# A delta rule loop of two steps a turn, with buffers by parity in place of copies

## The chip, the cores and the metric

The kernel runs on one core of one Trainium2 chip. The metric is the device time of one execution in microseconds; the median of several runs is given. TensorE is the matmul engine (PE in the profile, PEld for its weight loads), VectorE is DVE, ScalarE is ACT, GpSimd is POOL, and SyncE (SP) issues the DMAs of the part that is changed.

## What is computed

One layer of a bidirectional sequence mixer, followed by an MLP, over 2048 latent tokens with a prefix of 256 context tokens. The change touches one of the mixer's two head groups, the gated delta rule with 8 heads of width 64. It is computed in chunks of 64 tokens, for a forward and a backward direction:

```
gam = cumsum(log_g); dec = exp(gam_i - gam_j) for i >= j
a = (beta k) k^T * dec_strict + I                  # per chunk, 64 x 64
u = a^-1 (v beta); w = a^-1 (beta k exp(gam))
qk = (q k^T) * dec_incl
def step(s, xs):                                   # 36 chunks one after the other
    v_new = u - w s
    o = (q exp(gam)) s + qk v_new
    s = g_last * s + (k exp(gam_last - gam))^T v_new
```

The 256 context tokens and the 2048 latent tokens together make 36 chunks (NCH) in each direction.

## The kernel before

The program runs its phases one after the other: input norm and modulation, the input projection, the delta rule (`phase_gdn`), the other head group (HGRN), and then merge, output projection and MLP. Each engine has its own instruction list, and they synchronise by semaphores; within an engine everything runs in the order of its list.

`phase_gdn` handles one chunk a step, for all 8 heads and both directions at once, in tiles of 128 partitions by 512 numbers of fp32 (`W`). A matmul group in it is 16 matmuls of 64x64x64 in the code; the profile lists each group as 32 matmuls and 32 weight loads. The inverse of the triangular matrix is grown by levels: a `product` (a transposition of the inverse so far, and N times the inverse) on TensorE, a `take` from PSUM to SBUF on ScalarE (`g_txs`), a `grown` on TensorE, and a masked copy into the inverse on VectorE (`grow_block`, COPY_PREDICATED). Levels 0, 1 and the product of level 2 belong to the step n of the chunk; the rest of level 2, and levels 3 and 4 (`late_product`, `late_take`, `late_grown`, `late_block`), are done for chunk m = n - 1 while chunk n runs its early levels. Beside them, chunk m has its state work: `kv` (transposes keys and values), `ks` and `qs` (keys and queries times the state), `tz` (the inverse times the residual), `kdvn` (the update of the state) and `amvn` (the output).

Because two chunks are in work at once, ScalarE copies what chunk n+1 would overwrite: `nn` to `nn2` (hand_nn), `tt` to `tt2` (hand_tt), `tt2` to `ttb` (keep_inverse), values out of PSUM to `vt` (vtake), and `am` to `amb` (keep_am, three instructions, two of which also swap partition halves). GpSimd prepares the decay factors of chunk n+1 (`gaps`, `seeds`) from `grow`, a row that SyncE fetches with four DMAs (`load_rows`).

The steps are driven by `steps`: bodies 0, 35 and 36 are written out, and bodies 1 to 34 are one body in a loop (`eng.Fori(0, NCH - 2)`) with one step a turn. Every engine has its own copy of this loop, and waits in it compare a semaphore with a register that grows with the turn (`at`).

The names that the texts below use: in the profile, L1077, L1087, L1097, L1107, L1118 and L1129 are the matmuls of the helpers `to_tokens`, `to_channels`, `turn`, `across`, `back` and `keyed`.

Of the kernel before, what the change touches and what calls it, by code (L numbers as in the profile page):

```python
# [926 lines left out]
def at(i, n0, per, c):  # L927

    return n0 * per + c if i is None else i * per + (n0 * per + c)


def phase_gdn(nc, e):

    with nc.cleanup_on_exit(), ExitStack() as ctx:
# [11 lines left out]
        kqa, kqvb = sb("g_kqa", [P, 2, 2, PAIRS, CH]), sb("g_kqvb", [P, 2, 3, PAIRS, CH])  # L946
# [3 lines left out]
        nn, nn2, tt, tt2, ttb, am, amb = (sb("g_" + n, [P, *W]) for n in ("nn", "nn2", "tt", "tt2", "ttb", "am", "amb"))  # L950
        txs, txs2 = sb("g_txs", [P, 2, *W]), sb("g_txs2", [P, 2, *W])
        kd, vt, z, vn, o1, o, s, s1 = (sb("g_" + n, [P, *W]) for n in ("kd", "vt", "z", "vn", "o1", "o", "s", "s1"))
# [11 lines left out]
        nn2_ready, tt2_ready, ttb_ready, amb_ready = sem("g_nn2"), sem("g_tt2"), sem("g_ttb"), sem("g_amb")  # L964
        z_half, z_ready, o1_ready, o_ready, s_ready = sem("g_zh"), sem("g_z"), sem("g_o1"), sem("g_o"), sem("g_s")
        vt_ready, vn_ready, exp_ready, s1_ready = sem("g_vt"), sem("g_vn"), sem("g_exp"), sem("g_s1")
# [29 lines left out]
        def steps(eng, first, body):  # L996

            first()
            body(None, 0, True, False, True)
            with eng.Fori(0, NCH - 2) as i:  # L1000
                body(i, 1, True, True, True)
            body(None, NCH - 1, True, True, False)
            body(None, NCH, False, True, False)

        def chunks(i, n):

            if i is None:
                return n, NCH + CCH - 1 - n
            return i + n, i * (-1) + (NCH + CCH - 1 - n)

        with nc.Block() as block:
            @block.sync
            def _(sp):
# [15 lines left out]
                def load_kqvb(i, n):  # L1029
                    for g in range(2):  # L1030
                        src = e.skqv[:, ds(chunks(i, n)[g], 1)]
                        sp.dma_start(kqvb[:, g].rearrange("p (c j) a t -> p c (j a t)", c=1),
                                     src.rearrange("p c j t -> p c (j t)")).then_inc(kqvb_in, 16)
# [6 lines left out]
                def first():  # L1040
# [10 lines left out]
                    load_kqa(None, 0)  # L1051

                def body(i, n, a, c, pre):
# [15 lines left out]
            def _(pe):  # L1069
# [103 lines left out]
                def body(i, n, a, c, pre):  # L1173
                    m = n - 1

# [8 lines left out]
                    def product(l):  # L1184
# [7 lines left out]
                        turn(side(pa, 1), tile(tt))  # L1192
                        to_channels(side(pa, 0), tile(nn), tile(tt)).then_inc(tx_done, 1)
# [7 lines left out]
                    def late_product(l):  # L1201

                        pe.wait_ge(pred2_done, at(i, m, 3, l - 2))
                        pe.wait_ge(nn2_ready, at(i, m, 1, 1))
                        pe.sem_inc(go, 1)
                        turn(side(pc, 1), tile(tt2))
                        to_channels(side(pc, 0), tile(nn2), tile(tt2)).then_inc(tx2_done, 1)
# [13 lines left out]
                    def kv():  # L1221
                        pe.wait_ge(kqvb_in, at(i, m, 32, 32))
                        pe.wait_ge(s_ready, at(i, m, 1, 1))
                        pe.sem_inc(go, 1)
                        turn(side(pd, 0), chan(kqvb, 0), 1)
                        turn(side(pd, 1), chan(kqvb, 2)).then_inc(kv_turned, 1)

                    def ks():
                        pe.wait_ge(o_ready, at(i, m, 1, 1))
                        pe.sem_inc(go, 1)  # L1230
                        to_tokens(side(pb, 0), chan(kqvb, 0), of_state).then_inc(ks_done, 1)

                    def qs():
                        pe.wait_ge(vt_ready, at(i, m, 1, 1))
                        pe.sem_inc(go, 1)
                        to_tokens(side(pd, 0), chan(kqvb, 1), of_state, False).then_inc(qs_done, 1)

                    def tz():
                        pe.wait_ge(pred2_done, at(i, m, 3, 3))
                        pe.wait_ge(z_ready, at(i, m, 1, 1))  # L1240
                        pe.sem_inc(go, 1)
                        across(side(pb, 1), tile(ttb), tile(z)).then_inc(tz_done, 1)
# [11 lines left out]

                    if a:
                        gram()
                    if c:
                        kv()
                        late_grown(2)
                        late_product(3)  # L1260
                    if a:
                        product(0)
                    if c:
                        late_grown(3)
                        ks()
                    if a:
                        grown(0)
# [3 lines left out]
                    if a:  # L1271
                        product(1)
                    if c:
                        late_grown(4)
                    if a:
                        grown(1)
                    if c:
                        tz()
                    if a:
                        product(2)  # L1280
                    if c:
                        kdvn()
# [4 lines left out]
            def _(act):  # L1287
# [31 lines left out]
                def body(i, n, a, c, pre):  # L1319
# [10 lines left out]
                    def keep_am():  # L1330
# [3 lines left out]
                        nc.scalar.activation(amb[:, :, 0:2, :], am[:, :, 0:2, :], ACT.Copy)  # L1334
                        nc.scalar.activation(amb[halves(1), :, 2:4, :], am[halves(0), :, 2:4, :], ACT.Copy)
                        nc.scalar.activation(amb[halves(0), :, 2:4, :], am[halves(1), :, 2:4, :], ACT.Copy).then_inc(amb_ready, 1)
# [7 lines left out]
                    def hand_nn():  # L1344
                        act.wait_ge(nn_ready, at(i, n, 1, 1))
                        if c:
                            act.wait_ge(tx2_done, at(i, m, 2, 2))
                        nc.scalar.activation(nn2[:, :, :, :], nn[:, :, :, :], ACT.Copy).then_inc(nn2_ready, 1)

                    def hand_tt():  # L1350
                        act.wait_ge(pred_done, at(i, n, 2, 2))
                        nc.scalar.activation(tt2[:, :, :, :], tt[:, :, :, :], ACT.Copy).then_inc(tt2_ready, 1)

                    def vtake():
                        act.wait_ge(kd_ready, at(i, m, 1, 1))
                        nc.scalar.activation(heads_first(vt), pd[:, :, 1], ACT.Copy).then_inc(vt_ready, 1)
# [5 lines left out]
                    if c:  # L1362
                        keep_am()
                        vtake()
                        late_take(3)
                    if a:
                        take(0)
                    if pre:
                        distances(i, n + 1)
                    if c:  # L1370
                        keep_inverse()
                    if pre:
                        decays(i, n + 1)
                    if c:
                        late_take(4)
                    if a:
                        take(1)
                        hand_nn()
                    if c:
                        vntake()  # L1380
                    if a:
                        hand_tt()
# [4 lines left out]
            def _(pool):  # L1387
                def gaps(i, n):
                    nc.gpsimd.tensor_copy(cola[:, :, :, :].unsqueeze(2), colq[:, 0:3, ds(i + n if i is not None else n, 1)])\
# [17 lines left out]
                def take_colb(i, n):  # L1407
                    st = i + n if i is not None else n
# [12 lines left out]
                def body(i, n, a, c, pre):  # L1421
                    m = n - 1
                    if c:
# [3 lines left out]
                    if a:  # L1427
                        pool.wait_ge(tt_half, at(i, n, 1, 1))
# [1923 lines left out]
```

## Time and profile before

| | us |
|---|---|
| median of 3 runs (3765.59 to 3772.26) | 3768.53 |
| the profiled execution, its own time | 3773.59 |
| its span | 3771.8 |
| delta rule phase, bodies 0 to 36 (1081 to 1703) | 622 |
| of it the loop of one step a turn from its second turn on (1121.0 to 1660.9) | 539.9 |

The span is what the profile of one execution covers; the time of that execution is 1.8 us longer. Over the span the matmuls are busy for 87% of the time, VectorE for 53%, ScalarE for 44% and GpSimd for 45%. In the delta rule phase no engine is above 80%. A count such as x32 in a row of the timeline is the number of matmuls merged into it, "idle before" is how long the engine had nothing to do ahead of the row, and what stands behind the arrow is what ended that idle time; "issue" there means that the profile shows nothing that the engine waited for.

### The profile page before, as it was taken

How to read it: one execution, taken by the hardware profiler on the slowest of the kernel's cores; microseconds unless marked ns; L12 is line 12 of the kernel's file. 1: busy time of each engine (PE TensorE's matmuls, PEld its weight loads, DVE VectorE, ACT ScalarE, POOL GpSimd, SP SyncE). 2: the span in 40 equal slices, each digit the busy share in tenths (PEclk: the TensorE clock that was granted, in tenths of full speed). 3: DMA queues.
4: the chain of work that ended last, by engine and by line, in shares of the span. 5: the costliest groups of instructions: out<-in, count | busy, mean ns of one | idle time of the engine just before them, and what ended most of it. 6: DMA issues, size and time to landing. Idle time of an engine off the chain costs nothing. (4 is left out here: it accounts for less than half of the span.)

```text
span 3771.8 us, 114554 instructions
## 1 busy us (share of the span) xinstructions
PE 3270.4 (87%) x49145; PEld 2736.9 (73%) x49145; DVE 1995.1 (53%) x2896; ACT 1669.3 (44%) x2453; POOL 1715.4 (45%) x1364
## 2 busy tenths in 40 slices
PE   6899999999968788775677566999999999999998
PEld 3677888888857777764666535878877887787877
DVE  5488510111025555555666667665565546657575
ACT  5566422442135565552444424564454453323243
POOL 0211222333035555532666337546646656656564
PEclk8899999999979999995877867999999999999999
DMA  5133443353233333324433365766675666645453
GB/s 199 48 68 73 101 101 95 107 139 114 70 99 112 112 114 113 109 86 116 114 103 91 134 211 183 234 228 197 199 249 173 204 204 248 245 161 220 177 223 123
DMA packets 438348, 555.94 MB, mean 147 GB/s; under 512 B 119788, under 2 KB 355664, under 8 KB 413656
## 3 DMA queue, kind: packets, MB, share of 16 engines
q1 hardware_dynamic: 411936, 514.10, 42.7%
q10 hardware_dynamic: 20536, 21.58, 1.7%
q0 software_dynamic: 5632, 16.78, 1.5%
q8 instruction: 180, 2.95, 0.3%
q14 instruction: 64, 0.52, 0.0%
HBM read 354.42 MB, written 197.97 MB: 146 GB/s over the span
## 5 line engine op out<-in xcount | busy, mean ns | idle before, releaser
L3015 PE MATMUL o_pg<-o_t_hi,o_s_hi 128*128 128x512 f32 x2016 | 793.4, 394 | 47.1 <-ACT o_part L3062 13.0
L3017 PE MATMUL o_pg<-o_t_lo,o_s_hi 128*128 128x512 f32 x2016 | 790.2, 392 | 0.0
L3018 PE MATMUL o_pg<-o_t_hi,o_s_lo 128*128 128x512 f32 x2016 | 789.9, 392 | 0.0
L600 PE MATMUL p_pg<-h_hi,p_whi 128*128 128x512 f32 (+1 forms) x1384 | 531.6, 384 | 9.5 <-DVE p_wlo L827 9.5
L600 PE MATMUL p_pg<-h_lo,p_whi 128*128 128x512 f32 (+1 forms) x1384 | 519.4, 375 | 0.0
L600 PE MATMUL p_pg<-h_hi,p_wlo 128*128 128x512 f32 (+1 forms) x1384 | 519.3, 375 | 0.0
L3015 PEld LDWEIGHTS o_pg<-o_t_hi,o_s_hi 128*128 128x128 f32 x2016 | 381.8, 189 | 137.7 <-DVE o_s_lo L3222 35.7
L3018 PEld LDWEIGHTS o_pg<-o_t_hi,o_s_lo 128*128 128x128 f32 x2016 | 381.9, 189 | 80.1
L3017 PEld LDWEIGHTS o_pg<-o_t_lo,o_s_hi 128*128 128x128 f32 x2016 | 381.7, 189 | 78.7
L3222 DVE TENSOR_TENSOR o_s_lo<-o_raw,o_s_hi 128x512 fp32r<-128x512 f32 x288 | 267.5, 931 | 202.6 <-ACT o_s_hi L3051 202.6
L600 PEld LDWEIGHTS p_pg<-h_hi,p_whi 128*128 128x128 f32 x1384 | 262.4, 190 | 61.0 <-DVE p_wlo L827 9.8
L600 PEld LDWEIGHTS p_pg<-h_lo,p_whi 128*128 128x128 f32 x1384 | 262.5, 190 | 51.2 <-issue 5.5
L600 PEld LDWEIGHTS p_pg<-h_hi,p_wlo 128*128 128x128 f32 x1384 | 262.2, 189 | 47.0
L3051 ACT ACTIVATE o_s_hi<-o_raw 128x512 fp32r<-128x512 f32 x288 | 179.9, 625 | 227.4 <-PE o_pg L3018 215.0
L3222 DVE TENSOR_TENSOR o_s_lo<-o_mix,o_s_hi 128x512 fp32r<-128x512 f32 x216 | 209.2, 968 | 123.5 <-ACT o_s_hi L3051 123.5
L2948 POOL TENSOR_TENSOR o_xf<-o_xf,o_part 128x512 f32<-128x512 f32 x90 | 158.4, 1760 | 252.0 <-DVE o_part L3212 206.8
L808 ACT ACTIVATE p_y<-p_pg 128x512 f32<-128x512 f32 (+1 forms) x108 | 96.7, 895 | 379.0 <-PE p_pg L600 294.1
L674 POOL TENSOR_SCALAR p_macc<-p_mw,sc 128x512 f32<-128x512 f32 x8 | 13.7, 1717 | 530.7 <-PE p_pg L620 528.4
L3051 ACT ACTIVATE o_s_hi<-o_mix 128x512 fp32r<-128x512 f32 x216 | 135.4, 627 | 213.3 <-PE o_pg L3018 199.3
L2931 POOL TENSOR_TENSOR o_mix<-o_raw 128x512 f32<-128x512 f32 x72 | 101.2, 1406 | 188.7 <-DVE o_s_lo L3222 131.1
L1932 PE MATMUL b_pf<-b_qp,b_ks 64*64 64x32 f32 x3072 | 142.9, 252 | 49.4 <-ACT b_ax L2047 30.3
L823 DVE TENSOR_TENSOR p_wlo<-p_raw,p_whi 128x1024 fp32r<-128x1024 f32 x37 | 48.1, 1300 | 244.3 <-ACT p_whi L693 241.0
(334 smaller groups left out, 6669.3 us busy)
## 6 DMA issues: line engine op xcount, KB each, us to landing
o_raw<-in_w_mlp SPq DMA_DIRECT2D x32, 1024.0 KB, 6.4
scr_f<-o_xf SPq DMA_DIRECT2D x64, 512.0 KB, 8.1
o_raw<-scr_f SPq DMA_DIRECT2D x32, 1024.0 KB, 5.3
scr_w<-o_pre SPq DMA_DIRECT2D x16, 1792.0 KB, 7.1
o_t_raw<-scr_w SPq DMA_DIRECT2D x28, 1024.0 KB, 4.9
g_kqvb<-scr_kqv SPq DMA_DIRECT2D x72, 384.0 KB, 3.5
o_xf<-scr_x SPq DMA_DIRECT2D x22, 1024.0 KB, 7.7
p_raw<-in_w_in SPq DMA_DIRECT2D x38, 512.0 KB, 5.8
```

The lines of the kernel that those rows point to most:

```text
L600: last = nc.tensor.matmul(pg[0:m, bank, 0:n], w[:, q, k, 0:m], h[bank][:, k, :], start=(k == 0 and j == 0), stop=(k == KT - 1 and j == 2))
L674: nc.gpsimd.tensor_scalar(macc[:, :], w, sc, None, ALU.mult).then_inc(m_part, 1)
L808: last = nc.scalar.activation(put(yrow[u]), src, f)
L823: dve.tensor_tensor(wlo[:, q, :, 0:m], raw[:, q, :, 0:m], whi[:, q, :, 0:m].bitcast(F32), ALU.subtract).then_inc(w_lo, 1)
L1932: nc.tensor.matmul(pf[x, g, h, 0:HD // 2], ks[g][p][lo, h, x], ahead, start=True, stop=True)
L2931: nc.gpsimd.tensor_tensor(mix[:, 0], a21, a22, ALU.add).then_inc(mixed, 1)
L2948: nc.gpsimd.tensor_tensor(t, t, part[:, src], ALU.add).then_inc(x_added, 1)
L3015: nc.tensor.matmul(out, s_hi[:, q, k, :], t_hi[:, q, k, :], start=(not more and k == 0), stop=False, skip_group_check=more)
L3017: nc.tensor.matmul(out, s_hi[:, q, k, :], t_lo[:, q, k, :], start=False, stop=False, skip_group_check=more)
L3018: last = nc.tensor.matmul(out, s_lo[:, q, k, :], t_hi[:, q, k, :], start=False, stop=(k == 3), skip_group_check=more)
L3051: nc.scalar.activation(s_hi[:, q], operand(i, q), ACT.Copy).then_inc(s_hi_ready, 1)
L3222: dve.tensor_tensor(s_lo[:, q], operand(i, q), s_hi[:, q].bitcast(F32), ALU.subtract).then_inc(s_lo_ready, 1)
```

## The change

Eight edits, all in `phase_gdn`:

- The loop has two steps a turn and 16 turns. Bodies 0, 1, 34, 35 and 36 are now written out, and the loop covers 2 to 33. `at` and `chunks` count two steps a turn.
- `nn`, `tt`, `am` and `kqvb` become two buffers each, taken by the parity of the chunk. `nn2`, `tt2`, `ttb` and `vt` go, and with them four ScalarE instructions a step: hand_nn, hand_tt, keep_inverse and vtake.
- `residual_end` on VectorE subtracts the values straight from PSUM (`pd[:, :, 1]`).
- On TensorE the late level comes first in a step: `late_grown(2)` stands ahead of `gram`, `ks` ahead of `kv`, and `kdvn` ahead of `product(2)`; `grown(0)`, `product(1)` and `grown(1)` each come one place later against the late groups.
- ScalarE does `distances` and `decays` ahead of `take(0)`, and `keep_am` behind `late_take(4)`.
- GpSimd starts a step with `gaps`, and does the scaled state `s1` behind `seeds`.
- SyncE fetches `kqvb` first in a step and the decay rows `grow` two steps ahead.
- VectorE starts a step with `late_block(2)`, and `decay` waits for `tz_done` of the chunk two back, `attend` for `amb_ready` of the chunk two back.

```diff
 def at(i, n0, per, c):
-    return n0 * per + c if i is None else i * per + (n0 * per + c)
+    return n0 * per + c if i is None else i * (2 * per) + (n0 * per + c)
...
-        nn, nn2, tt, tt2, ttb, am, amb = (sb("g_" + n, [P, *W]) for n in ("nn", "nn2", "tt", "tt2", "ttb", "am", "amb"))
+        nn, tt, am = ([sb(f"g_{n}{p}", [P, *W]) for p in range(2)] for n in ("nn", "tt", "am"))
+        amb = sb("g_amb", [P, *W])
...
             first()
             body(None, 0, True, False, True)
-            with eng.Fori(0, NCH - 2) as i:
-                body(i, 1, True, True, True)
+            body(None, 1, True, True, True)
+            with eng.Fori(0, (NCH - 4) // 2) as i:
+                body(i, 2, True, True, True)
+                body(i, 3, True, True, True)
+            body(None, NCH - 2, True, True, True)
             body(None, NCH - 1, True, True, False)
             body(None, NCH, False, True, False)
...
                 def body(i, n, a, c, pre):
+                    if a:
+                        if i is not None or n > 1:
+                            sp.wait_ge(qs_done, at(i, n, 1, -1))
+                        load_kqvb(i, n)
                     if pre:
-                        sp.wait_ge(d_ready, at(i, n, 1, 1))
-                        load_rows(i, n + 1)
+                        if i is not None or n < NCH - 2:
+                            sp.wait_ge(d_ready, at(i, n, 1, 2))
+                            load_rows(i, n + 2)
                         sp.wait_ge(kkq_done, at(i, n, 1, 1))
                         load_kqa(i, n + 1)
-                    if a:
-                        if c:
-                            sp.wait_ge(qs_done, at(i, n, 1, 0))
-                        load_kqvb(i, n)
...
                     def qs():
-                        pe.wait_ge(vt_ready, at(i, m, 1, 1))
+                        pe.wait_ge(z_ready, at(i, m, 1, 1))
...
-                    def keep_inverse():
-                        act.wait_ge(pred2_done, at(i, m, 3, 2))
-                        if i is not None or m:
-                            act.wait_ge(tz_done, at(i, m, 1, 0))
-                        nc.scalar.activation(ttb[:, :, :, :], tt2[:, :, :, :], ACT.Copy).then_inc(ttb_ready, 1)
...
                     def residual_end():
                         dve.wait_ge(z_half, at(i, m, 1, 1))
-                        dve.wait_ge(vt_ready, at(i, m, 1, 1))
-                        dve.tensor_tensor(z[:, :, :, :], z[:, :, :, :], vt[:, :, :, :], ALU.subtract).then_inc(z_ready, 1)
+                        dve.wait_ge(kv_turned, at(i, m, 1, 1))
+                        dve.tensor_tensor(heads_first(z), heads_first(z), pd[:, :, 1], ALU.subtract).then_inc(z_ready, 1)
```

Three places show the instructions as they stand in the built program; the change has line numbers of its own, in which L1085, L1095, L1105, L1115, L1126 and L1137 are the matmuls of `to_tokens`, `to_channels`, `turn`, `across`, `back` and `keyed`. The first is TensorE at the end of a turn of the delta rule loop. Before, after `product(2)`, `kdvn` and `amvn` (L1129, L1118) the engine branches back; what follows is the written-out body 35:

```order
L1190 REGISTER_ALU
L1097 MATMUL g_pa<-cst,g_tt 64x64 x16
L1087 MATMUL g_pa<-g_tt,g_nn 64x64 x16
L1129 MATMUL g_pd<-g_vn,g_kd 64x64 x16
L1118 MATMUL g_pb<-g_vn,g_amb 64x64 x16
L1000 REGISTER_ALU
L1000 COMPARE_AND_BRANCH
L1077 MATMUL g_pa<-g_kqa 64x64 x32
L1097 MATMUL g_pd<-cst,g_kqvb 64x64 x32
```

In the change, the same end of a step in the middle of a turn runs on into the second step without a branch:

```order
L1199 REGISTER_ALU
L1105 MATMUL g_pa<-cst,g_tt 64x64 x16
L1095 MATMUL g_pa<-g_tt,g_nn 64x64 x16
L1126 MATMUL g_pb<-g_vn,g_amb 64x64 x16
L1221 REGISTER_ALU
L1085 MATMUL g_pc<-g_txs 64x64 x16
L1186 REGISTER_ALU
L1085 MATMUL g_pa<-g_kqa 64x64 x32
L1105 MATMUL g_pc<-cst,g_tt 64x64 x16
```

The branch stands only behind the second step, and the written-out body 34 follows it:

```order
L1199 REGISTER_ALU
L1105 MATMUL g_pa<-cst,g_tt 64x64 x16
L1095 MATMUL g_pa<-g_tt,g_nn 64x64 x16
L1126 MATMUL g_pb<-g_vn,g_amb 64x64 x16
L1003 REGISTER_ALU
L1003 COMPARE_AND_BRANCH
L1085 MATMUL g_pc<-g_txs 64x64 x16
L1085 MATMUL g_pa<-g_kqa 64x64 x32
```

A turn of this loop had 24 matmul groups on TensorE between the two ends of its branch, and has 48 now.

The second place is TensorE at the start of a step. Before, it runs `gram`, `kv`, `late_grown(2)` and `late_product(3)`:

```order
L1077 MATMUL g_pa<-g_kqa 64x64 x32
L1222 REGISTER_ALU
L1223 REGISTER_ALU
L1097 MATMUL g_pd<-cst,g_kqvb 64x64 x32
L1077 MATMUL g_pc<-g_txs 64x64 x16
L1203 REGISTER_ALU
L1097 MATMUL g_pc<-cst,g_tt 64x64 x16
L1087 MATMUL g_pc<-g_tt,g_nn 64x64 x16
```

In the change, it runs `late_grown(2)`, `gram`, `late_product(3)`, `ks` and `kv`:

```order
L1085 MATMUL g_pc<-g_txs 64x64 x16
L1186 ISA
L1085 MATMUL g_pa<-g_kqa 64x64 x32
L1212 REGISTER_ALU
L1105 MATMUL g_pc<-cst,g_tt 64x64 x16
L1095 MATMUL g_pc<-g_tt,g_nn 64x64 x16
L1235 REGISTER_ALU
L1236 ISA
L1085 MATMUL g_pb<-g_s,g_kqvb 64x64 x16
L1105 MATMUL g_pd<-cst,g_kqvb 64x64 x32
L1225 ISA
L1085 MATMUL g_pc<-g_txs 64x64 x16
```

The first group of a step is now one of 16 matmuls on `g_txs`, and `ks` (g_pb from the state) moved from behind `late_grown(3)` to ahead of `kv`.

The third place is ScalarE in the second half of a step. Before, the two takes are followed by the copy of `nn` (L1348), the take of `vn`, the copy of `tt` (L1352) and the last take:

```order
L1327 REGISTER_ALU
L1328 ACTIVATE g_txs<-g_pc 128x1024
L1323 REGISTER_ALU
L1324 ACTIVATE g_txs<-g_pa 128x1024
L1348 ACTIVATE g_nn<-g_nn 128x512
L1360 ACTIVATE g_vn<-g_pb 128x512
L1351 REGISTER_ALU
L1352 ACTIVATE g_tt<-g_tt 128x512
L1323 REGISTER_ALU
L1324 ACTIVATE g_txs<-g_pa 128x1024
```

In the change, the three `amb` instructions stand between the two takes and both copies are gone:

```order
L1335 REGISTER_ALU
L1336 ACTIVATE g_txs<-g_pc 128x1024
L1339 REGISTER_ALU
L1341 REGISTER_ALU
L1343 ACTIVATE g_amb<-g_am 128x2x128
L1344 ACTIVATE g_amb<-g_am 64x2x128
L1345 ACTIVATE g_amb<-g_am 64x2x128
L1331 REGISTER_ALU
L1332 ACTIVATE g_txs<-g_pa 128x1024
L1349 ACTIVATE g_vn<-g_pb 128x512
L1331 REGISTER_ALU
L1332 ACTIVATE g_txs<-g_pa 128x1024
```

## Rows read from the trace of the kernel before

**Rows 1.** Busy time by stretch, in us, with instruction counts and granted clock

```profile
core 0: us, PE busy (x) PEld busy (x) DVE busy (x) ACT busy (x) POOL busy (x), PEclk, DMA share, GB/s
...
1099.70:1121.00 21.30, 13.89 (x779) 12.96 (x773) 9.87 (x19) 9.86 (x15) 8.79 (x10) 0.98 0.21 66
1121.00:1660.90 539.90, 431.66 (x25287) 403.12 (x25280) 315.52 (x626) 322.65 (x494) 289.52 (x329) 1.00 0.36 112
1660.90:1683.90 23.00, 13.97 (x771) 12.75 (x771) 9.45 (x21) 9.41 (x14) 2.68 (x5) 1.00 0.16 50
```

**Rows 2.** Timeline of TensorE, one warm turn: start us, duration us, instruction

```profile
1398.87 1.16 PE L1077 MATMUL g_pa<-g_kqa 64*64 64x64 f32 x64 [0.31 <-ACT g_txs L1324]
...
1403.41 0.68 PE L1097 MATMUL g_pa<-cst,g_tt 64*64 64x64 f32 x32
...
1411.04 0.69 PE L1077 MATMUL g_pa<-g_txs 64*64 64x64 f32 x32 [0.22 <-ACT g_txs L1324]
...
1412.69 0.69 PE L1097 MATMUL g_pa<-cst,g_tt 64*64 64x64 f32 x32 [0.23 <-DVE g_tt L1487]
1413.18 0.68 PE L1087 MATMUL g_pa<-g_tt,g_nn 64*64 64x64 f32 x32
...
1415.10 1.16 PE L1077 MATMUL g_pa<-g_kqa 64*64 64x64 f32 x64 [0.31 <-ACT g_txs L1324]
```

**Rows 3.** Waits in the warm loop: total us, times, longest us

```profile
PE g_pc L1077 <- ACT g_txs L1328: 50.8, 66, 1.4
PE g_pc L1097 <- DVE g_tt L1498: 30.9, 33, 0.9
PE g_pa L1077 <- ACT g_txs L1324: 17.1, 65, 0.3
PE g_pa L1097 <- DVE g_tt L1487: 7.0, 33, 0.2
...
POOL g_dd L1395 <- DMA g_grow<-scr_gam: 127.1, 33, 4.3
```

**Rows 4.** Groups by line in the loop: busy us, mean ns

```profile
L1512 DVE TENSOR_TENSOR g_z<-g_z,g_vt 128x512 f32<-128x512 f32 x35 | 39.0, 1114 | 0.0
...
L1342 ACT ACTIVATE g_ttb<-g_tt 128x512 f32<-128x512 f32 x35 | 21.5, 615 | 2.7 <-DVE g_tt L1498 2.7
```

**Rows 5.** DMA queues of 1099:1120, 1140:1660 and 1660:1703 in turn

```profile
q8 instruction: 5, 0.08, 1.7%
...
DMA packets 62159, 58.47 MB, mean 112 GB/s; under 512 B 37839, under 2 KB 45775, under 8 KB 62159
...
q1 hardware_dynamic: 62159, 58.47, 36.5%
...
q8 instruction: 9, 0.15, 1.5%
```

**Rows 6.** Timeline of TensorE in the loop's first turn

```profile
1107.31 0.52 PE L1077 MATMUL g_pa<-g_txs 64*64 64x64 f32 x20 [0.75 <-issue]
...
1111.53 0.62 PE L1097 MATMUL g_pa<-cst,g_tt 64*64 64x64 f32 x25 [2.13 <-issue]
...
1119.12 0.69 PE L1118 MATMUL g_pb<-g_vn,g_amb 64*64 64x64 f32 x30 [1.52 <-issue]
```

**Rows 7.** Timeline of TensorE in body 35, written out behind the loop

```profile
1669.92 0.33 PE L1077 MATMUL g_pb<-g_s,g_kqvb 64*64 64x64 f32 x2 [1.30 <-issue]
1670.03 0.69 PE L1077 MATMUL g_pa<-g_txs 64*64 64x64 f32 x32
...
1671.45 0.66 PE L1077 MATMUL g_pd<-g_s,g_kqvb 64*64 64x64 f32 x28
1673.61 0.33 PE L1077 MATMUL g_pd<-g_s,g_kqvb 64*64 64x64 f32 x4 [1.49 <-issue]
...
1677.59 0.34 PE L1077 MATMUL g_pa<-g_txs 64*64 64x64 f32 x5 [0.81 <-issue]
...
1682.69 0.34 PE L1129 MATMUL g_pd<-g_vn,g_kd 64*64 64x64 f32 x7 [2.29 <-issue]
```

More of the change, by code:

```diff
@@ L945, in phase_gdn @@
         glq = sb("g_glq", [P, NCH, 2 * PAIRS])
-        kqa, kqvb = sb("g_kqa", [P, 2, 2, PAIRS, CH]), sb("g_kqvb", [P, 2, 3, PAIRS, CH])
+        kqa = sb("g_kqa", [P, 2, 2, PAIRS, CH])
+        kqvb = [sb(f"g_kqvb{p}", [P, 2, 3, PAIRS, CH]) for p in range(2)]
         grow = sb("g_grow", [P, *W])
@@ L1191, in product @@
                         pe.sem_inc(go, 1)
[L1192 to L1193 removed]
+                        turn(side(pa, 1), tile(tt[p]))
+                        to_channels(side(pa, 0), tile(nn[p]), tile(tt[p])).then_inc(tx_done, 1)
                     def grown(l):
@@ L1257, in body @@
                     if c:
-                        kv()
-                        late_grown(2)
-                        late_product(3)
+                        late_product(3)
+                        ks()
+                        kv()
+                        late_grown(3)
                     if a:
                         product(0)
[L1263 to L1267, printed above, removed]
                     if c:
@@ L1271, in body @@
                     if a:
-                        product(1)
+                        grown(0)
                     if c:
@@ L1275, in body @@
                     if a:
-                        grown(1)
+                        product(1)
                     if c:
@@ L1279, in body @@
                     if a:
+                        grown(1)
+                    if c:
+                        kdvn()
+                    if a:
                         product(2)
                     if c:
-                        kdvn()
                         amvn()
@@ L1407, in take_colb @@
                 def take_colb(i, n):
-                    st = i + n if i is not None else n
+                    st = i * 2 + n if i is not None else n
                     nc.gpsimd.tensor_copy(colb[:, :, :, :].unsqueeze(2), colq[:, Q_KDEC:Q_REST, ds(st, 1)])
@@ L1422, in body @@
                     m = n - 1
+                    if pre:
+                        gaps(i, n + 1)
+                    if a:
+                        pool.wait_ge(tt_half, at(i, n, 1, 1))
+                        pool.wait_ge(c_ready, at(i, n, 1, 1))
+                        nc.gpsimd.tensor_tensor(tt[n % 2][:, :, :, :], tt[n % 2][:, :, :, :], c2[:, :, :, :], ALU.add).then_inc(tt_init, 1)
+                    if pre:
+                        pool.wait_ge(tt_init, at(i, n, 1, 1))
+                        seeds(i, n + 1)
                     if c:
@@ L1533, in body @@
                     if a:
+                        decay()
                         attend()
                     if c:
+                        residual()
+                        late_block(3)
                         keys()
-                        late_block(3)
-                        residual()
+                        residual_end()
                     if a:
@@ L1541, in body @@
                     if c:
-                        residual_end()
+                        late_block(4)
                         carried()
-                        late_block(4)
                     if a:
```

107 lines of the change are left out of this document (39 added, 68 removed).

## The prediction, written before the change was run

> **What bounds the kernel now.** Only the delta rule phase changes, so I read the stretches of it first, from the view of busy time by stretch [rows 1]. The reader is to see three lines. The loop's first turn takes 21.3 us. The 33 turns behind it take 539.9 us, 16.36 us each. The written-out body 35 takes 23.0 us, for the same work: about 770 matmuls and 770 weight loads in all three (25287 over 33 is 766). TensorE's clock was granted in full in the last two (1.00) and nearly so in the first (0.98), and the DMA share is lowest where the step is slowest. So a step has a warm price and a cold one, some 5 to 7 us apart, and neither clock nor data traffic explains it.
>
> The second view is the timeline of one warm turn [rows 2]. From one `gram` to the next are 16.23 us (1398.87 to 1415.10). No engine is full: a matmul group occupies TensorE for 0.47 to 0.49 us (1412.69 to 1413.18), so the 24 groups are some 11.4 us. The rest are waits, and the table of waits says which: TensorE waits for the take of the late level 50.8 us in total, for the masked copy of the late level 30.9, for the early take 17.1 and for the early masked copy 7.0 [rows 3], 105.8 us or 3.2 us a turn. The warm turn is thus a chain of dependences across TensorE, ScalarE and VectorE, with the order of TensorE's list woven in. GpSimd's 127.1 us of waiting for the decay rows [rows 3] are not in that chain: `gram` waits for the last take on ScalarE in both turns shown [rows 2].
>
> The third view is the DMA queues of three stretches [rows 5], with the cold timelines beside it [rows 6, 7]. In the first turn an instruction queue (q8) moved 5 packets of 16 KB, and behind the loop 9. In 520 us of the warm loop all 62159 packets are data (q1): no code was fetched at all. And the cold timelines show what the fetch does to TensorE: it stops in the middle of a group, with nothing to wait for ("issue"), goes on, and stops again one block later. From 1669.92 to the next stop I count 2+32+32+32+28 = 126 matmuls, each with a weight load (the two groups between the rows shown are like 1670.03), so a block is some 254 instructions of these and a couple of semaphore waits. The resumptions are 11.81 us apart over three blocks in the first turn (1107.31 to 1119.12) [rows 6] and 12.77 us over three in body 35 (1669.92 to 1682.69) [rows 7]: **4.10 us a block on average**, the shortest 3.69. Blocks come one at a time and no earlier than that. Warm, TensorE goes through a block in 16.36 / 6.1 = 2.7 us. So TensorE's code is held near the engine while the loop runs, and outside it arrives slower than it is executed.
>
> **The change, part by part.** *The doubled turn.* A step is 768 / 126 = 6.1 blocks of TensorE's code. One step a turn was held; two are 12.2, and as a stretch of 12.2 rarely begins and ends at an edge, 13 blocks. Whether 13 blocks are held no row shows; this is the unknown that decides, and I bound it from both sides. Held: nothing is fetched after the first turn. Not held: if blocks leave in the order in which they came, a turn that is longer than the store finds none of its own code, and every turn is as cold as the first. I take the second. What is shown held is 6.1 blocks (7 with the edges), and 540 us of an idle fetch queue did not bring in the code behind the loop: body 35, begun at 1660.9 [rows 1], stands still until 1669.92, 1673.61, 1677.59 and 1682.69, block after block [rows 7]. A store with room for twice the loop had the time to hold it.
>
> The cold turn then costs 13 x 4.10 = 53.3 us, and I add 1 us for the branch back, since the block fetched ahead there is the one behind the loop (between 0 and a whole fetch of 4.1). That is 54.3 us for two steps. Sixteen turns: 869 us. The same 32 steps took 32 x 16.36 = 523.5. **+345 us.**
>
> The Trainium skill, "Runtime: NRT & Kernel Launch", section "Instruction fetch mechanics", gives TensorE's instruction memory as 128 KiB, 2048 instructions, a FIFO refilled in blocks of 256. By it the two steps (over 3,070 matmuls and loads) are not held and the one step was; the trace agrees with the block and with the held single step. The same section also says that there are only two lines of 16 KiB and that a branch to anything further back stalls; by that the loop before would have fetched six blocks in each turn, 25 us instead of 16.36, and here the trace contradicts it.
>
> *More written-out bodies.* Body 1 is as cold as the loop's first turn was. Body 34 was the last warm turn and is now written out: 22 us (between 21.3 and 23.0) less 16.4, **+6 us**. Bodies 0, 35 and 36 stay as they are.
>
> *The four copies.* They cost ScalarE about 0.6 us each (615 ns for `ttb`) [rows 4], 2.4 us a step, and `vtake` and the copy of `nn` stand ahead of takes that TensorE waits for. `residual_end` goes from 1114 ns [rows 4] to that of its neighbours, some 0.7. *The new order* starts the late level at once. Worth together, warm: from `product(0)` to the next `gram` are 11.69 us (1403.41 to 1415.10) [rows 2]. Without anything in their way, product and take are 2.41 (1412.69 to 1415.10) and grown and masked copy 1.65 (1411.04 to 1412.69); three of the first and two of the second are 10.53. With 0.3 for `grown(0)` behind `qs` it is 10.8, a gain of 0.85 a step. The part ahead of `product(0)` stays near 4.5 us: five groups, the masked copy between and the late take. In the cold turn all this is worth nothing: the chain of about 15.5 us a step has 27.1 us to run in, beside the stops for code. So I put it at **0**; without that cover it is -0.85 x 32 = -27.
>
> *Decay rows two steps ahead* removes GpSimd's wait, which nobody waits for: 0. The new `d_ready` wait on SyncE has the two `kqa` loads of the next chunk queued behind it, for which `gram` waits; they issue some 10 us before they are needed in so long a turn. The waits on the chunk two back (`tz_done`, `amb_ready`) are for work a whole step old: 0.
>
> Sum: +345 + 6 = +351 us on the profiled execution's 3773.6 (span 3771.8 and 1.8 around it), 4125. The median of the runs is 5.1 us lower, so **4120 us**.
>
> **The rivals.**
> 1. *All 13 blocks are held* (not slower). For it: no row shows where the store ends. Then two of 32 steps are cold and 30 warm: -0.85 x 30 = -26 us; cold steps added are 2, 3 and 34 at some 5.3 us, +16. Together -10 us, 3759 us. It decides at a single number: from 13 blocks of room upwards this holds, at 12 it does not. If the new order gains nothing, 3785, slower after all. Chance 0.12, of it 0.07 faster, 0.03 the same, 0.02 slower.
> 2. *Part is held*: something like half of the turn is kept and 6 blocks are fetched. Then a turn is 6 x 4.10 + 6.2 x 2.7 = 41.3 us against 32.7; 16 x 8.6 + 6 = +144, 3912 us. Against it: this needs a store that does not lose its blocks in order. Chance 0.06.
> 3. *The refetch as forecast*, 0.82. Its own range: at best 12.2 blocks at 3.69 and nothing at the branch, 45.0 us a turn, +197 + 5, 3970. At worst the 4.26 of body 35 and a whole fetch at the branch, 59.5 us a turn, +428 + 7, 4204; and if a third of the 3.2 us of waits for data came on top of the stops, +34 more, about 4240.
>
> **How the numbers follow.** 4120 is the refetch. 3970 to 4240 would hold it nearly always; I reach down to 3910 for the second rival, which makes some 0.82 in all. About 0.2%, 7.5 us, is what a measurement of this kernel tells from no change. Faster 0.07, same 0.03, slower 0.82 + 0.06 + 0.02 = 0.90.
>
> **What would show it.** The instruction queue should show 13 packets in each turn of the loop, some 200 where there were none; the timeline should show TensorE stopping with "issue" ahead of it, in mid-group, every 126 or so matmuls, about 4.1 us apart; the loop's 32 steps should take 870 us, at 27 us each, and no wait for a take should be the longest. ScalarE's four copies are gone, and GpSimd no longer waits for the decay rows. I am wrong if the warm turns show no instruction packets: then the time is near 3760, and the chain of takes and masked copies decides. I am wrong in size if blocks arrive faster than 3.7 us apart when they are asked for in a steady row, or if the branch back costs a fetch of its own.

## The result, and the profile after

The changed kernel takes 4178.41 us (median of 4 runs, 4176.79 to 4179.98) against 3770.4 us before in the same comparison: a ratio of 1.1082, 95% interval [1.1063, 1.1102]. It is 408 us slower. The prediction was 4120 us, in a range of 3910 to 4240.

The busy time by stretch of the changed kernel, to be read against [rows 1] (us, counts, granted TensorE clock, DMA share, GB/s): the written-out body 1, 15 turns of the loop (all but the first), body 34, body 35.

```profile
core 0: us, PE busy (x) PEld busy (x) DVE busy (x) ACT busy (x) POOL busy (x), PEclk, DMA share, GB/s
1097.90:1119.40 21.50, 15.50 (x768) 14.23 (x769) 8.47 (x18) 7.89 (x11) 8.34 (x10) 0.92 0.11 29
1172.60:2038.60 866.00, 523.43 (x23058) 484.95 (x23049) 277.03 (x570) 242.08 (x330) 251.15 (x300) 0.80 0.23 68
2039.70:2063.80 24.10, 16.61 (x768) 15.51 (x768) 9.38 (x20) 8.02 (x11) 7.16 (x8) 0.86 0.21 69
2063.80:2089.50 25.70, 15.98 (x768) 14.73 (x768) 8.39 (x20) 6.63 (x9) 3.65 (x5) 0.90 0.15 45
```

Fifteen turns take 866.0 us, 57.73 us each and 28.9 us a step, where a step took 16.36 [rows 1]. The matmuls are the same, 1537 a turn for twice 768. No turn is warm any more. A step in the loop even costs more than the cold bodies before and behind it, 28.9 us against 21.5, 24.1 and 25.7. The DMA queues of the same 15 turns:

```profile
q1 hardware_dynamic: 58560, 55.07, 21.3%
q8 instruction: 210, 3.44, 1.8%
```

These are 210 packets of code, 14 a turn, where the warm loop before had none [rows 5]. TensorE's waits in these turns (total us, times, longest):

```profile
PE g_pc L1085 <- issue: 71.4, 15, 5.0
PE g_pa L1095 <- issue: 61.7, 45, 2.4
PE g_pa L1085 <- issue: 61.6, 44, 2.3
PE g_pd L1105 <- issue: 53.6, 29, 3.6
...
PE g_pa L1105 <- DVE g_tt L1471: 11.4, 30, 0.5
PE g_pc L1085 <- ACT g_txs L1332: 8.2, 15, 0.8
```

The long waits of [rows 3], for the takes on ScalarE and the masked copies on VectorE, have shrunk to some 10 us each. In their place stands "issue", which is TensorE having no instruction. The first row is a kind of its own: it comes 15 times, once a turn, with 4.76 us each. The timeline shows both kinds; here are the first row of a turn, the rows of its second half ahead of which TensorE had stood still, and at the end the first row behind the branch back:

```profile
1294.32 1.13 PE L1085 MATMUL g_pc<-g_txs 64*64 64x64 f32 x32 [4.86 <-issue]
...
1323.98 0.58 PE L1085 MATMUL g_pa<-g_kqa 64*64 64x64 f32 x9 [1.00 <-issue]
...
1328.87 0.85 PE L1105 MATMUL g_pd<-cst,g_kqvb 64*64 64x64 f32 x42 [1.55 <-issue]
...
1332.59 0.39 PE L1095 MATMUL g_pa<-g_tt,g_nn 64*64 64x64 f32 x11 [1.62 <-issue]
...
1336.21 0.40 PE L1085 MATMUL g_pa<-g_txs 64*64 64x64 f32 x12 [1.49 <-issue]
...
1339.82 0.47 PE L1115 MATMUL g_pb<-g_z,g_tt 64*64 64x64 f32 x17 [0.82 <-issue]
...
1344.31 0.50 PE L1095 MATMUL g_pa<-g_tt,g_nn 64*64 64x64 f32 x18 [1.64 <-issue]
...
1349.98 0.50 PE L1085 MATMUL g_pc<-g_txs 64*64 64x64 f32 x8 [4.64 <-issue]
```

As in [rows 6, 7], the stops fall into the middle of groups, here 3.6 to 4.9 us apart. Then, behind the branch, TensorE stands for 4.64 us, in which it does nothing at all. That stop is the fetch of the turn's first block. The other twelve come while the turn runs: in the turn shown, the twelve distances from 1294.32 to 1344.31 are 4.17 us on average, and the last one, over the branch, is 5.67. Read in the same way over 14 turns, which are 57.8 us long on average, a turn is **12 x 4.33 + 5.8**; the 5.8 are 1.0 us of work on the last block and 4.8 of standing still. The fourteenth packet is one more than the blocks that a turn uses; I take it for the block behind the loop, fetched ahead and never used.

The rest of the change did what it says. In the groups by line GpSimd's wait for the decay rows is gone (127.1 us in [rows 3], 7.5 now, behind a copy of its own), and the subtraction straight from PSUM takes VectorE 0.68 us where the one from `vt` took 1.11 [rows 4]:

```profile
L1378 POOL TENSOR_TENSOR g_dd<-g_grow,g_cola 128x512 f32<-128x512 f32 x33 | 34.4, 1043 | 7.5 <-POOL g_cola L1372 7.4
...
L1491 DVE TENSOR_TENSOR g_z<-g_z,g_pd 128x512 f32<-128x512 f32 x35 | 23.7, 677 | 0.0
```

### The profile page after: what moved, and what is told of

Its sections match the earlier page's. It is cut to its first block and busy times, and to the rows that moved or that the text cites. A ratio compares the mean times of both kernels' runs of the same rounds, so it can differ in the third digit from the quotient of the medians.

```text
span 4175.0 us, 113800 instructions
## 1 busy us (share of the span) xinstructions
PE 3404.8 (82%) x49145; PEld 2854.8 (68%) x49145; DVE 1986.4 (48%) x2896; ACT 1605.1 (38%) x2309; POOL 1697.2 (41%) x1364
## 5 line engine op out<-in xcount | busy, mean ns | idle before, releaser
L2993 PEld LDWEIGHTS o_pg<-o_t_hi,o_s_hi 128*128 128x128 f32 x2016 | 380.9, 189 | 140.0 <-DVE o_s_lo L3200 35.9
L1332 ACT ACTIVATE g_txs<-g_pa 128x1024 f32<-128x1024 f32 x108 | 110.6, 1024 | 401.3 <-PE g_pa L1095 401.3
L1411 POOL TENSOR_TENSOR g_tt<-g_tt,g_c 128x512 f32<-128x512 f32 x36 | 46.0, 1277 | 429.0 <-DVE g_tt L1459 429.0
L1336 ACT ACTIVATE g_txs<-g_pc 128x1024 f32<-128x1024 f32 x72 | 73.8, 1025 | 292.2 <-PE g_pc L1095 292.2
```

What stands on the lines that cost most here:

```text
L1332: nc.scalar.activation(txs[:, :, :, :, :], pa[:, :, :, :, :], ACT.Copy).then_inc(tx_ready, 1)
L1336: nc.scalar.activation(txs2[:, :, :, :, :], pc[:, :, :, :, :], ACT.Copy).then_inc(tx2_ready, 1)
L1411: nc.gpsimd.tensor_tensor(tt[n % 2][:, :, :, :], tt[n % 2][:, :, :, :], c2[:, :, :, :], ALU.add).then_inc(tt_init, 1)
L2993: nc.tensor.matmul(out, s_hi[:, q, k, :], t_hi[:, q, k, :], start=(not more and k == 0), stop=False, skip_group_check=more)
```

## The experiments

### Two steps a turn and nothing else

The kernel before, with its buffers, its copies and its order, and only the loop doubled:

```diff
-            with eng.Fori(0, NCH - 2) as i:
-                body(i, 1, True, True, True)
+            body(None, 1, True, True, True)
+            with eng.Fori(0, (NCH - 4) // 2) as i:
+                body(i, 2, True, True, True)
+                body(i, 3, True, True, True)
+            body(None, NCH - 2, True, True, True)
```

> The kernel before with the two-step turn alone: one set of buffers, the four ScalarE copies and the old order of every engine kept; bodies 1 and 34 written out. Theory (TensorE's code of two steps isn't held, and each block is fetched again each turn): the turn costs what it costs in the changed kernel, 57.7 us, whatever the order in it, so 4150 to 4200 us, with 13 to 14 instruction packets a turn. Rival (a good part of the loss comes from the new order, the new waits or the parity buffers): clearly faster than the changed kernel, below 4100, and near 3790 if the doubling itself is harmless (only the written-out bodies).

Measured: 4126.79 us, ratio 1.0943 [1.0926, 1.096]. The stretch of 15 turns, and the code packets in it:

```profile
1169.20:1989.20 820.00, 493.20 (x23048) 456.40 (x23042) 296.01 (x570) 306.82 (x450) 259.13 (x300) 0.84 0.24 71
...
q8 instruction: 210, 3.44, 1.9%
```

The same 210 packets, and 54.67 us a turn. The doubling alone thus costs 355 us of the 408. The expected 4150 us was missed from below: the changed kernel has 3.06 us a turn, about 50 us, which this one has not. It does not lie at the branch. Here are the first row of a turn, its last resumption ahead of the branch and the first row behind it:

```profile
1284.33 1.98 PE L1080 MATMUL g_pa<-g_kqa 64*64 64x64 f32 x64 [4.93 <-issue]
...
1332.72 0.50 PE L1132 MATMUL g_pd<-g_vn,g_kd 64*64 64x64 f32 x17 [0.82 <-issue]
...
1338.45 1.99 PE L1080 MATMUL g_pa<-g_kqa 64*64 64x64 f32 x64 [4.71 <-issue]
```

Over the branch it is 5.73 us, as in the changed kernel, and the twelve distances ahead of it are 4.03 us on average (over 14 turns 5.8 and 4.07). So the 3 us lie in the twelve blocks that come while the turn runs, 4.33 us apart in the changed kernel and 4.07 here. The last two experiments look for the reason.

### The new order with one step a turn

The changed kernel with one set of buffers and the copies hand_nn, hand_tt and keep_inverse put back, and the loop over bodies 1 to 33. Two things stand as before the change: SyncE fetches `kqvb` last in a step, and `keep_am` comes first on ScalarE.

```diff
-            body(None, 1, True, True, True)
-            with eng.Fori(0, (NCH - 4) // 2) as i:
-                body(i, 2, True, True, True)
-                body(i, 3, True, True, True)
+            with eng.Fori(0, NCH - 3) as i:
+                body(i, 1, True, True, True)
             body(None, NCH - 2, True, True, True)
```

> The new order of all engines, decay rows two steps ahead and the subtraction straight from PSUM, but one step a turn and one set of buffers, so that three of the four ScalarE copies stay; body 34 written out. Theory (the loss is the code alone; the order is worth 0.85 us a step once the code is held): 33 warm steps save 28 us, one more cold body costs 6, about 3748 us, no instruction packets in the loop. Rival (the new order itself lengthens the step): over 3780 us. If the gain lay in the copies and not in the order, 3770 to 3780.

Measured: 3753.55 us, ratio 0.9953 [0.994, 0.9967]. 32 warm turns take 501.4 us, 15.67 each:

```profile
1118.20:1619.60 501.40, 421.92 (x24597) 395.79 (x24595) 296.90 (x608) 305.27 (x448) 269.57 (x320) 1.00 0.38 117
```

The new order, together with leaving out the take of `vt`, is a gain of 0.7 us a step once the code is held, and it needs neither the parity buffers nor the second step in a turn.

### Where the store ends: five, ten and two groups more

The kernel before, with k more matmul groups in the body of the loop; they write the same numbers to the same place:

```diff
+                        for _ in range(k if i is not None else 0):
+                            turn(side(pd, 0), chan(kqvb, 0), 1)
                         turn(side(pd, 0), chan(kqvb, 0), 1)
```

> The kernel before with five more matmul groups in the loop's body (the transposition of the keys done six times over into the same place): 29 groups instead of 24, 7.4 blocks of code instead of 6.1. Theory with a store of 8 blocks: still held, no instruction packets, and the time grows by at most 5 x 0.47 us x 34 = 80 us: 3810 to 3855 us. If the store ends below 8 blocks: every turn refetches 8 blocks and pays one more fetch at the branch, 8 x 4.1 + 4.5 = 37 us a step, +700 us, 4470.

> The same with ten more groups: 34 groups, 8.7 blocks of code. Store of 8 blocks that loses them in the order in which they came: nothing is held, 9 x 4.1 + 4.5 = 41 us a step, +820 us, about 4600, and 9 to 10 instruction packets a turn. A store of 12 blocks: held, +160 us at most, 3880 to 3930, no packets. A store that keeps a part: one to three packets a turn, 3950 to 4100.

> The kernel before with two more matmul groups in the loop's body: 26 groups, 6.6 blocks of code, which lie in 7 blocks as those of the kernel before do. Theory (held are the blocks of the loop and one ahead, 8 in all): no instruction packets, and at most 2 x 0.47 us a step, 3772 to 3805 us. Rival (the repeated transpositions themselves made the kernel with five groups slow): +200 us.

Measured, one run each: 4308.73 us with five groups, 4430.02 with ten, 3787.55 with two. The stretches of 33 turns with five groups and with ten, each with its code packets:

```profile
1122.20:2196.50 1074.30, 641.41 (x30643) 594.87 (x30638) 316.33 (x628) 339.16 (x495) 290.44 (x330) 0.85 0.21 61
...
q8 instruction: 297, 4.87, 2.1%
```

```profile
1128.80:2312.80 1184.00, 717.22 (x35920) 664.46 (x35918) 299.34 (x628) 338.92 (x496) 287.83 (x330) 0.90 0.19 56
...
q8 instruction: 329, 5.39, 2.0%
```

With two groups, the 33 turns, and the DMA packets of 32 of them, which are all data:

```profile
1119.70:1671.80 552.10, 455.25 (x27469) 431.77 (x27462) 315.53 (x628) 327.66 (x496) 287.12 (x330) 1.00 0.36 110
```

```profile
DMA packets 62464, 58.74 MB, mean 110 GB/s; under 512 B 37888, under 2 KB 46080, under 8 KB 62464
...
q1 hardware_dynamic: 62464, 58.74, 35.7%
```

26 groups (832 matmuls and as many loads a turn, 6.6 blocks) are held: 16.73 us a turn. 29 groups (7.4 blocks) are not: 9 packets and 32.55 us a turn. Three groups, which are 1.4 us of TensorE's time, make the turn twice as long. My expectation for five groups had been that 8 blocks are held; the edge is one block lower. There is no middle either: one block too many, and all of them are fetched again in every turn. Only TensorE's code was made longer, so it is TensorE's code that q8 brings, and the kernel with two groups repeats the same transposition and is not slow, so the repetition itself is not the reason. The price of a cold turn was overestimated, 37 and 41 us against 32.55 and 35.9 (10 packets a turn). The expectation counted the turn's first block twice, once at 4.1 us and once as the stop at the branch. With the 5.8 us over the branch, the rest of a turn is 7 distances of 3.8 us with five groups and 8 of 3.8 with ten.

### Four steps a turn, and no loop at all

The changed kernel with `body(i, 2)` to `body(i, 5)` in 8 turns (`at`, `chunks` and the columns count four), and with all bodies written out:

```diff
+            for n in range(1, NCH - 1):
+                body(None, n, True, True, True)
```

> The changed kernel with four steps a turn (8 turns). Nothing held in either case; what differs is how often the branch back is paid. Theory (a block costs 4.09 us, the branch one fetch of 4.6 us with nothing beside it): a turn is 25 x 4.09 + 4.6 = 106.9 us, 26.7 a step where the changed kernel has 28.9, -69 us: about 4110. Rival (the doubling costs by the size of the turn, the branch nothing): no change, 4178, or slower.

> The changed kernel with all 37 bodies written out, no branch. Theory: 6.13 blocks a step at 4.09 us are 25.1 us, 3.8 less than now over 32 steps, -120 us: about 4057, still 290 us above the kernel before, and this is the price of the blocks alone. Rival (the branch is the main cost): near 3800.

Measured: 4128.73 us and 4084.61 us, one run each. Seven turns of four steps, and then 814 us of the written-out kernel with its code packets:

```profile
1229.00:1995.60 766.60, 486.75 (x21515) 451.55 (x21512) 257.80 (x532) 224.81 (x309) 233.67 (x280) 0.81 0.24 71
```

```profile
1146.00:1960.00 814.00, 509.57 (x24304) 468.87 (x24300) 291.65 (x600) 252.29 (x346) 264.76 (x316) 0.88 0.26 76
```

```profile
q8 instruction: 192, 3.15, 1.6%
```

A turn of four steps is 109.5 us, 27.4 a step: two turns of the changed kernel (115.5) less 6 us, which is the one crossing of the branch that is saved: 24 x 4.32 + 5.8. Without any branch the blocks come 4.24 us apart (814 / 192), and the kernel is 94 us faster than the changed one; the 15 stops of 4.76 at the branch were 71 us. Both came out some 20 to 30 us above what was expected, because the expectations took a block at 4.09 us, where this order of work has 4.33 in the loop of two steps, 4.32 in that of four and 4.24 without one. The loss of some 312 us that is left without a loop is the price of the blocks in this order.

### Half of the matmuls in the loop

Both kernels with half of each helper's matmuls left out in the loop, which brings two steps to 6.2 blocks. This is the one way tried to run two steps a turn, with the parity buffers, from held code:

```diff
-                    for g in range(2):
+                    for g in range(G[0]):
...
+                    G[0] = 2 if i is None else 1
```

> The kernel before with half of the matmuls left out in the loop (each helper does only one of its two directions; all waits and all work of the other engines stay); body 1 written out. It leaves out part of the computation. Held as before, no packets. The chain of takes and masked copies stays and the groups shrink from 0.47 to 0.24 us: 15.1 us a step instead of 16.4, about 3735.

> The changed kernel with the same half of the matmuls left out in its loop: two steps are then 6.2 blocks, as much code as one step before. It leaves out part of the computation. Theory (the code is the whole loss, the rest of the change is a gain): no instruction packets in the loop, and a step shorter than that of the half kernel before by 0.85 to 2.4 us, 3665 to 3715 us. Rival (waits, buffers or order of the change cost time of their own): slower than the half kernel before.

Measured: 3764.44 us before, 3701.89 us changed, one run each. 32 turns of one step, then 15 turns of two, and the packets of the last 14 of these, none of them on q8:

```profile
1137.00:1659.60 522.60, 362.70 (x12301) 325.99 (x12296) 301.11 (x608) 310.89 (x481) 281.14 (x320) 0.65 0.37 112
```

```profile
1153.90:1561.70 407.80, 290.30 (x11532) 253.97 (x11529) 271.04 (x571) 236.97 (x330) 251.03 (x300) 0.84 0.45 135
...
DMA packets 54657, 51.41 MB, mean 136 GB/s; under 512 B 33152, under 2 KB 40320, under 8 KB 54656
...
q1 hardware_dynamic: 54656, 51.40, 45.1%
...
q14 instruction: 1, 0.01, 0.0%
```

The changed loop fetched no code after its second turn and takes 13.6 us a step against 16.3. So two steps in a turn, with the parity buffers and the new waits, do not make the turn long when the code is held. The size of the gain is not to be read from this pair: with half the work TensorE's granted clock fell, to 0.65 in the one and 0.84 in the other, and a small cost of the buffers or waits could hide behind that. The lower clock is also the likely reason why the half kernel before did not get faster as expected (16.33 us a step and not 15.1); that was not tried.

### The decay rows one step ahead again

The kernel with the new order and one step a turn, `load_rows(i, n + 1)` as before the change, GpSimd's `gaps` behind the start of the inverse again, and ScalarE's distances and decays behind the second late take:

```diff
-            with eng.Fori(0, NCH - 3) as i:
+            with eng.Fori(0, NCH - 2) as i:
                 body(i, 1, True, True, True)
-            body(None, NCH - 2, True, True, True)
...
-                        if i is not None or n < NCH - 2:
-                            sp.wait_ge(d_ready, at(i, n, 1, 2))
-                            load_rows(i, n + 2)
+                        sp.wait_ge(d_ready, at(i, n, 1, 1))
+                        load_rows(i, n + 1)
```

> As the kernel with the new order and one step a turn (3753.6 us), but with the decay rows fetched one step ahead as before, so that body 34 is in the loop again, and ScalarE's distances and decays behind the second late take. Theory (the rows two ahead bring nothing; one cold body less): 3745 to 3749 us. Rival (the rows two ahead carried part of the gain): 3755 or more.

Measured: 3748.34 us, ratio 0.9928 [0.9914, 0.9941], the fastest of the kernels that do all the work. 33 turns, and TensorE's waits in them:

```profile
1118.80:1635.80 517.00, 435.47 (x25363) 406.90 (x25358) 310.09 (x627) 314.69 (x462) 275.95 (x330) 1.00 0.38 117
```

```profile
PE g_pc L1078 <- ACT g_txs L1326: 24.5, 32, 0.8
PE g_pa L1078 <- ACT g_txs L1326: 17.8, 33, 0.9
PE g_pc L1078 <- ACT g_txs L1330: 15.0, 33, 0.5
PE g_pa L1098 <- DVE g_tt L1484: 14.9, 33, 0.5
PE g_pc L1098 <- DVE g_tt L1495: 8.4, 33, 0.3
```

15.67 us a turn, the same as with the rows two ahead: fetching them earlier brings nothing that these orders of ScalarE and GpSimd do not bring as well. That this kernel is 5 us faster than the one with the rows two ahead is about what one cold body less gives. The waits add up to 80.6 us, 25 less than in [rows 3]; over 33 turns that is 0.76 us a step, and the step is 0.7 shorter.

### Why the changed turn is 3 us longer than two steps a turn alone

The changed kernel with SyncE's loads in the order of before, and the changed kernel with TensorE's groups in the order of before. In the first, GpSimd's `gaps` stay where the change put them, unlike what its expectation says; the edit is on SyncE alone:

```diff
-                    if a:
-                        if i is not None or n > 1:
-                            sp.wait_ge(qs_done, at(i, n, 1, -1))
-                        load_kqvb(i, n)
...
+                    if a:
+                        if c:
+                            sp.wait_ge(qs_done, at(i, n, 1, 0))
+                        load_kqvb(i, n)
```

> The changed kernel with SyncE's loads as before: decay rows one step ahead, kqvb behind kqa and after the queries' product, GpSimd's gaps behind the inverse's start. It asks why the changed kernel's turn (57.7 us) is 3 us longer than that of two steps a turn alone (54.7). Theory (all loads of a step in one burst slow the fetch of code that falls into it, 4.7 to 5.1 us a block there): 55 to 56 us a turn, 4130 to 4160. Rival (the order on TensorE is what costs in a cold turn): unchanged within 10 us of 4178.

> The changed kernel with TensorE's groups in the order of before, all else as changed (two steps a turn, parity buffers, loads in one burst). It asks what of the 3.0 us between the changed kernel's turn (57.7) and that of two steps a turn alone (54.7) lies in TensorE's order, after the loads' order accounted for 1.3. Theory: the rest is TensorE's order in a turn that waits for code; the turn falls to 56.0 us or less, 4125 to 4155. Rival (it lies in what remains: ScalarE's, VectorE's and GpSimd's order and the parity buffers): 4170 to 4185.

Measured: 4163.92 us, ratio 1.1028 [1.1011, 1.1044], with the old order of loads, and 4194.77 us, ratio 1.1109 [1.109, 1.1127], with the old order on TensorE. 15 turns of the first, and near 15 turns of the second:

```profile
1176.80:2023.10 846.30, 526.65 (x23060) 489.77 (x23056) 277.49 (x570) 243.10 (x331) 249.81 (x300) 0.79 0.23 69
```

```profile
1180.00:2050.00 870.00, 556.39 (x22738) 513.68 (x22739) 265.66 (x563) 237.11 (x325) 249.40 (x296) 0.75 0.23 67
```

What led me to the loads were two stretches of the changed kernel. In the first, where all loads of a step run at once, blocks came 4.9 us apart (1323.98 to 1328.87 above), in the second 3.6 us (1336.21 to 1339.82). But two more stretches of the same turn, shown behind them, do not fit: a block came after 4.0 us (1298.16 to 1302.16) at a DMA share of 0.56, and another after 4.4 us (1314.36 to 1318.79) at 0.01.

```profile
1324.00:1329.00 5.00, 3.45 (x134) 3.31 (x138) 2.58 (x4) 2.29 (x3) 3.42 (x4) 0.72 0.76 220
...
1337.00:1341.00 4.00, 2.51 (x138) 2.12 (x128) 1.80 (x6) 1.62 (x2) 1.58 (x4) 1.00 0.01 4
...
1298.00:1302.00 4.00, 3.69 (x126) 3.50 (x126) 1.93 (x4) 1.70 (x3) 3.32 (x3) 0.50 0.56 164
...
1314.00:1319.00 5.00, 2.87 (x137) 2.58 (x140) 1.43 (x3) 0.60 (x1) 0.00 (x0) 1.00 0.01 3
```

Spreading the loads gave 56.42 us a turn (846.3 / 15) and 14 us in all, of the 52 that were to be explained (19 us when each kernel is set against the kernel before of its own comparison). TensorE's old order gave nothing back; it cost 16 us more (12 in the same way). So the loads' order accounts for 1.3 of the 3.1 us, the theory on TensorE's order fell, and the rival named there, 4170 to 4185, was missed as well. What makes the other 1.8 us of a cold turn stays open. It can lie in the order of ScalarE, VectorE and GpSimd or in the parity buffers, none of which was put back alone. The granted clock differs too, 0.84 in the turns of 54.7 us, 0.80 in those of 57.7, 0.79 with the old order of loads and 0.75 with the old order on TensorE, but whether it is a cause or follows from how the stops lie was not tried.

## Why the prediction was right

**The bound.** The warm turn was the chain of takes and masked copies, as said. In the kernel with the new order and one step a turn these waits shrank by 25 us, and the 33 turns by 23 (539.9 to 517.0).

**The code.** The step that decided was right: 13 blocks are not held and each is fetched in each turn (14 packets a turn, the same with the doubling alone). The argument for it had only been that nothing beyond 6.1 blocks was shown held. The added groups have put the edge in its place: 6.6 blocks held, 7.4 not, so the rival of a held turn was far from true, and that of a turn held in part fell with it, since the turn of 7.4 blocks fetches all of its blocks.

The Trainium skill, "Runtime: NRT & Kernel Launch", section "Instruction fetch mechanics", gives TensorE an instruction memory of 2048 instructions, refilled in blocks of 256, which makes eight. The trace fits it if one of the eight belongs to the block ahead: a loop that lies in 7 blocks is held, and one of some 1,890 instructions, below 2048, is not. That the eighth is taken by the fetch ahead is argued from the extra packet in every turn (14 for 13 blocks, 9 for 8) and not shown by itself.

**The size of it.** A turn was put at 13 x 4.10 + 1 = 54.3 us, that is twelve distances of 4.10 and 5.1 over the branch. The doubling alone has 12 x 4.07 + 5.8 = 54.6, so this sum was right for it, with a branch 0.7 us too cheap and blocks a little too dear. The changed kernel has 12 x 4.33 + 5.8 = 57.8. The term that was off is therefore the one for the copies and the new order in a cold turn: it was put at 0, and against the doubling alone the rest of the change cost 3.06 us a turn, about 50 of the 58 us by which 4120 was too low. The doubling alone, at 4127 us, lies 7 us above the forecast: the branch adds about 11 us over fifteen crossings, and blocks that came a little faster than 4.10 take some 6 back.

The same section of the Trainium skill says that a taken branch whose target lies outside the current window of two pages forces a fetch of the target page before execution can continue. The window of two is not what this case shows, since a loop that lies in seven blocks turned without a fetch; the forced fetch is, in the loops that are not held, with 4.64 us at the branch.

**The written-out bodies.** Body 34 takes 24.1 us cold, put at 22, and body 35, put at no change, takes 25.7 where it took 23.0 [rows 1]. Both are 2 to 3 us too low; with the same new order of work this fits blocks that come further apart, but it was not tried.

**Copies and order at 0 under that cover.** Half right. The gain is indeed covered: the chain no longer bounds, and TensorE's waits for takes and masked copies are some 10 us each in 866. But the prediction saw no way in which the new order could cost anything in a cold turn, and there it cost 3 us, of which 1.3 come from the order of the loads and the rest is open. What the order is worth without the cover was put at 0.85 us a step, and 0.7 was measured with three of the four copies still there.

**Decay rows.** Right: the wait went, and nothing came of it.

## What to carry to other kernels

Before unrolling a loop to save copies, count the instructions of its largest engine in blocks of the instruction queue's packets, with the edges, and look whether the loop runs without such packets now: here every matmul group is 64 instructions, and a body of 26 groups ran warm while one of 29 took twice as long. Past that edge the time is that of the blocks as they come, 3.8 to 4.4 us apart here, plus 5.8 over each branch back, and of the orders of work tried in the loop of two steps none was faster than the old one: between them a turn took 54.7 to 59 us. An order that shortens the chain of waits is worth taking in the loop that is still held, and was, with 26 us. A turn of the loop that was seen cold, its first one, and a body behind the loop give the price of a block before anything is changed, but neither has the stop at the branch in it.

## What was not expected of the hardware

- The edge is sharp: with 6.6 blocks no code packet in 32 turns, with 7.4 blocks 9 a turn, for 16.7 and 32.6 us.
- At the branch back to code that is no longer held TensorE stands still for 4.4 to 5.0 us, with the new order as with the old: 4.76 us on average in the changed kernel and 4.77 with the doubling alone.
- In one turn, blocks come 3.4 to 5.2 us apart. One came after 4.9 us at a DMA share of 0.76 and one after 3.6 us at 0.01, but others after 4.0 us at 0.56 and 4.4 us at 0.01, so data traffic alone does not set the distance.
- Halving the matmuls of a held loop left its step at 16.3 us, with the granted clock at 0.65 instead of 1.00.
